# Attention's sixteen units set among the last pieces of the second block's input projection

## What is computed

```
h = rms_norm(x, g_mix_norm) * (1 + sc_m) + sh_m
proj = h @ w_in                       # 1024 -> 5704
q_a, k_a, v_a, q_i, k_i, w_i, q_b, k_b, v_b, gate_a, gate_b = split(proj)
q_a, k_a, q_b, k_b = rope(rms_norm(per head));  q_i, k_i = rope(...)
# DSA, 4 heads of 128: an indexer (8 heads of 64) scores each pair of tokens,
score = sum_h w_i[h] * relu(q_i[h] . k_i), causal;  keep the 64 best keys of each query
o_a = softmax(q_a k_a^T / sqrt(128) over the kept keys) v_a
# MoBA, 4 heads of 128: with 256 tokens there is one block, so it is plain causal attention
o_b = softmax(q_b k_b^T / sqrt(128), causal) v_b
merged = sigmoid(gate_a) * (o_a @ w_br_dsa) + sigmoid(gate_b) * (o_b @ w_br_moba)
x = x + gt_m * (merged @ w_out)
```

## Time and profile before

| | us |
|---|---|
| median of 3 runs | 1394.65 |
| the runs | 1391.75, 1394.65, 1402.45 |
| profiled execution, span from the first to the last instruction | 1392.0 |

### The profile page before, as it was taken

The page is one execution under the profiler, slowest core; times in us unless marked ns, Lnnn a source line. Parts: engine busy times, 40 slices in busy tenths (PEclk is TensorE's granted clock), DMA queues, the critical chain, the costliest instruction groups (busy, mean ns, idle before and its releaser), DMA issues. The chain is left out here.

```text
span 1392.0 us, 19967 instructions
## 1 busy us (share of the span) xinstructions
PE 1208.7 (87%) x7750; PEld 830.8 (60%) x7750; DVE 960.6 (69%) x2109; ACT 413.6 (30%) x879; POOL 276.3 (20%) x264
## 2 busy tenths in 40 slices
PE   4898998888888888888887777779999979999998
PEld 1887866654332423333242222338889869999998
DVE  0595336699787868878786875677776979566552
ACT  2661225321110111111001010136354464544431
POOL 0000000045344444434434343410000000000000
PEclk9899999989999999999999999999999989999999
DMA  9366069699999999999999999974656704566553
GB/s 394 154 235 192 8 243 429 276 410 419 421 421 421 422 421 421 422 420 414 421 411 415 421 402 423 420 323 194 242 189 235 285 18 152 212 235 244 188 201 132
DMA packets 50764, 428.29 MB, mean 308 GB/s; under 512 B 5744, under 2 KB 7920, under 8 KB 8304
## 3 DMA queue, kind: packets, MB, share of 16 engines
q0 software_dynamic: 36864, 268.45, 46.6%
q1 hardware_dynamic: 13808, 158.59, 29.3%
HBM read 423.64 MB, written 1.05 MB: 305 GB/s over the span
## 5 line engine op out<-in xcount | busy, mean ns | idle before, releaser
L1475 PE MATMUL bank<-arena 128*128 128x512 f32 x1024 | 497.7, 615 | 112.2 <-DVE arena L1646 111.8
L1475 PEld LDWEIGHTS bank<-arena 128*128 128x128 f32 x1024 | 177.4, 190 | 417.1 <-DVE arena L1646 274.5
L1710 DVE CUSTOM_DVE_ANT_0 arena<-arena 128x1024 f32<-128x1024 f32 x256 | 313.3, 1224 | 133.6 <-DMA arena<-experts_in,arena 132.5
L1380 POOL DMA_INDIRECT arena<-experts_in,arena x256 | 275.8, 1077 | 605.8 <-PE bank L1475 350.8
L562 PE MATMUL bank<-rounded,rounded 128*128 128x256 f32 x1264 | 372.5, 295 | 26.5 <-DVE rounded L519 13.5
L563 PE MATMUL bank<-rounded,rounded 128*128 128x256 f32 x1264 | 361.6, 286 | 0.0
L564 PE MATMUL bank<-rounded,ring_r 128*128 128x256 f32 x1264 | 361.2, 286 | 0.0
L537 DVE TENSOR_TENSOR ring_r<-ring,rounded 128x1024 fp32r<-128x1024 f32 (+2 forms) x155 | 194.6, 1263 | 113.1 <-ACT rounded L532 112.2
L562 PEld LDWEIGHTS bank<-rounded,rounded 128*128 128x128 f32 x1264 | 246.3, 195 | 34.9 <-issue 25.9
L563 PEld LDWEIGHTS bank<-rounded,rounded 128*128 128x128 f32 x1264 | 246.1, 195 | 3.8 <-issue 3.3
L564 PEld LDWEIGHTS bank<-rounded,ring_r 128*128 128x128 f32 x1264 | 246.0, 195 | 0.0
(11 more groups left out here) (282 smaller groups left out, 994.4 us busy)
## 6 DMA issues: line engine op xcount, KB each, us to landing
ring<-slots_in SPq DMA_DIRECT2D x68, 2048.0 KB, 8.5
arena<-slots_in SPq DMA_DIRECT2D x4, 2048.0 KB, 23.8
arena<-experts_in,arena POOLq DMA_INDIRECT x256, 13.6
xT<-xT_in SPq DMA_DIRECT2D x1, 1024.0 KB, 10.9
...
```

The lines of the kernel that those rows point to most:

```text
L1380: pool.indirect_dma_start(rows[:, r % GRING, :], None, experts_in, bass.IndirectOffsetOnAxis(ap=expert[:, tt, at:at + 1], axis=0)).then_in ...
L1475: ins = pe.matmul(psum[2 * tt + half][:, :], diag[:, r % DIAGS, :], rows[:, r % GRING, D + 512 * half:D + 512 * half + 512], start=(h == 0 ...
L1710: dve.tensor_tensor_reduce(rows[:, r % GRING, 0:D], rows[:, r % GRING, 0:D], utok[:, tt, :], 1.0, 0.0, ALU.mult, ALU.add, hdot[:, r:r + 1] ...
```

## The change

- The items are in another order: the indexer's q, k and weights first, then DSA's values, DSA's q, MoBA's values, DSA's k, MoBA's q and k; the gates stay last (27 to 42). Which columns of the weights lie in which slot is changed to match.
- The loop over items becomes a loop over 44 slices (45 on ACT). Index scores run in slices 9 to 16, the rounds of top-8 in slices 18 to 25, and the mask is made at the end of slice 25.
- Attention's block is gone. Unit u (DSA's are first now) has its logits in PE's slice 25+u, largest on DVE and exponents on ACT in slice 26+u, scaling and transpose in slice 27+u, copy and values in slice 28+u, and the last copy in slice 29+u.
- Items rotate through three banks (before four), all other products through five (before four).
- The gates are evicted with a plain copy. Behind the last item, Sigmoid is applied in place in two instructions of 128x2048. The branch block's DVE waits for them.
- The attention's result goes to `uT`, so that two copies of 128x1024 between `mixT` and `uT` (L1978, L2197) are gone. The first three pieces of the branch weights are prepared in slices 40 to 42.

```diff
-        items = [item("feat", 0, i * P, qk[:, i, :]) for i in range(4)]
-        items += [item("feat", 1, i * P, qk[:, 4 + i, :]) for i in range(4)]
+        items = [item("feat", 0, i * P, qki[:, i, :]) for i in range(4)]
+        items += [item("feat", 1, 0, qki[:, 4, :])]
+        items += [item("weight", 1, tt, wi[:, tt, :], scale=IDX_SCALE) for tt in range(TT)]
         items += [item("token", 2, tt, vtok[:, 0, tt, :]) for tt in range(TT)]
-        items += [item("feat", 3, i * P, qki[:, i, :]) for i in range(4)]
-        items += [item("feat", 4, 0, qki[:, 4, :])]
-        items += [item("weight", 4, tt, wi[:, tt, :], scale=IDX_SCALE) for tt in range(TT)]
-        items += [item("feat", 5, i * P, qk[:, 8 + i, :]) for i in range(4)]
-        items += [item("feat", 6, i * P, qk[:, 12 + i, :]) for i in range(4)]
-        items += [item("token", 7, tt, vtok[:, 1, tt, :]) for tt in range(TT)]
-        items += [item("feat", 8 + i // 4, (i % 4) * P, sgate[:, i, :], ACT.Sigmoid) for i in range(16)]
+        items += [item("feat", 3, i * P, qk[:, i, :]) for i in range(4)]
+        items += [item("token", 4, tt, vtok[:, 1, tt, :]) for tt in range(TT)]
+        items += [item("feat", 5, i * P, qk[:, 4 + i, :]) for i in range(4)]
+        items += [item("feat", 6, i * P, qk[:, 8 + i, :]) for i in range(4)]
+        items += [item("feat", 7, i * P, qk[:, 12 + i, :]) for i in range(4)]
+        items += [item("feat", 8 + i // 4, (i % 4) * P, sgate[:, i, :]) for i in range(16)]
...
+        score, left, relu = uT[:, 0:2, :], uT[:, 2:4, :], uT[:, 4:8, :]
+        maskd, max8 = area(27692, TT, T), area(28204, TT, 8)
+        NI = 16
+        nmax, psm, rsm = area(28220, NI), area(28236, NI), area(28252, NI)
+        sm, pT = area(21792, 4, T), area(4096, 2, T)
...
+        LAST_OF = [10, 12, 16, 18, 20, 22, 24, 26]
+        SUM_AFTER = {LAST_OF[p] + 1: p for p in range(NPAIR)}
+        ROOT_AFTER = {LAST_OF[p] + 2: p for p in range(NPAIR)}
+        NORM_AT = {LAST_OF[p] + 3: p for p in range(NPAIR)}
+        FLIP_AFTER = {2: 8, 4: 9, 6: 10, 14: 0, 16: 1, 20: 2, 22: 3, 24: 4, 26: 5, 28: 6, 30: 7}
+        TURN_AT = {4: 8, 6: 9, 8: 10, 16: 0, 18: 1, 22: 2, 24: 3, 26: 4, 28: 5, 30: 6, 32: 7}
         TURNS = [TURN_AT[t] for t in sorted(TURN_AT)]
-        DOTS = {5: (0, 1), 6: (1, 2), 8: (2, 4), 12: (4, 6), 13: (6, 8), 22: (8, 10), 25: (10, 12), 29: (12, 13),
-                30: (13, 14), 31: (14, 15), 32: (15, 16), 33: (16, 17), 34: (17, 18), 35: (18, 19), 36: (19, 20)}
-        FIRST_SCORE = 29
-        AUX = {}
-        for n in range(NITEM):
+        QI_EVICTED = {8: 2, 9: 4, 10: 5}
+        DOTS = {5: (0, 1), 6: (1, 2), 7: (2, 3), 9: (3, 4), 10: (4, 6), 11: (6, 8)}
+        DOTS.update({26 + j: (8 + j, 9 + j) for j in range(12)})
+        FIRST_SCORE, FIRST_ROUND, FIRST_UNIT = 9, 18, 25
+        AUX_BANK, NAUX = 3, 5
...
+        def what(u):
+            b, h, tt = u // 8, u // 2 % 4, u % 2
+            return b, h, tt, width[tt]
+        wbr = Split([(SLOTS["w_br"][0] + n // 8, D, (n % 8) * P, n) for n in range(16)], 4, uT, 22816, sem("br_mm"),
+                    x_at=17696)
+        br_mm = wbr.mm
...
+                def logits(u):
+                    b, h, tt, w = what(u)
+                    bank = aux_bank("logit", u)
+                    pe.wait_ge(hr["fin"], TURNS.index(4 * b + 2 + h // 2) + 1)
+                    pe.matmul(bank[:, 0:w], qk[:, 8 * b + h, tt * P:(tt + 1) * P], qk[:, 8 * b + 4 + h, 0:w],
+                              start=True, stop=True).then_inc(at["s"], 1)
+
+                def shares_turned(u):
+                    b, h, tt, w = what(u)
+                    bank = aux_bank("turn", u)
+                    pe.wait_ge(at["p"], u + 1)
+                    for st_ in range(tt + 1):
+                        ins = pe.transpose(bank[:, st_ * P:(st_ + 1) * P], sm[:, u % 4, st_ * P:(st_ + 1) * P], ident)
+                    ins.then_inc(at["t"], 1)
+
+                def values(u):
+                    b, h, tt, w = what(u)
+                    bank = aux_bank("value", u)
+                    pe.wait_ge(at["pT"], u + 1)
+                    for st_ in range(tt + 1):
+                        ins = pe.matmul(bank[:, 0:P], vtok[:, b, st_, h * HD:(h + 1) * HD],
+                                        pT[:, u % 2, st_ * P:(st_ + 1) * P], start=(st_ == 0), stop=(st_ == tt))
+                    ins.then_inc(at["o"], 1)
...
+                for n in range(PLAIN, NSLICE):
+                    if n < NITEM:
+                        kind, s, col, *_ = items[n]
+                        if items[n - 1][1] != s:
+                            wait_slot(pe, W2[s])
+                        if n >= 3:
+                            pe.wait_ge(i2_ev, n - 2)
+                        bank, w = psum[n % 3], slot(W2[s])
...
+                    u = n - FIRST_UNIT
+                    if 0 <= u < NI:
+                        logits(u)
+                    if 0 <= u - 2 < NI:
+                        shares_turned(u - 2)
+                    if 0 <= u - 3 < NI:
+                        values(u - 3)
...
+                def exponents(u):
+                    w = what(u)[3]
+                    act.wait_ge(at["max"], u + 1)
+                    act.activation(sm[:, u % 4, 0:w], sm[:, u % 4, 0:w], ACT.Exp, bias=nmax[:, u:u + 1],
+                                   accum_out=psm[:, u:u + 1]).then_inc(at["exp"], 1)
+
+                def shares_out(u):
+                    w = what(u)[3]
+                    act.wait_ge(at["t"], u + 1)
+                    if u >= 2:
+                        act.wait_ge(at["o"], u - 1)
+                    act.copy(pT[:, u % 2, 0:w], aux("turn", u)[:, 0:w]).then_inc(at["pT"], 1)
+
+                def values_out(u):
+                    b, h, tt, w = what(u)
+                    act.wait_ge(at["o"], u + 1)
+                    act.copy(uT[:, 4 * b + h, tt * P:(tt + 1) * P], aux("value", u)[:, 0:P]).then_inc(at["oT"], 1)
 
                 mix2_norm.act(act, wi2, rooted=True, late=True)
-                for n, (kind, s, col, dst, func, scale) in enumerate(items):
-                    if n >= PLAIN and n + LEAD in i2_feat:
+                for n in range(NSLICE + 1):
+                    if PLAIN <= n and n + LEAD in i2_feat:
                         wi2.act_hi(act, i2_feat.index(n + LEAD) - PLAIN)
-                    act.wait_ge(i2_mm, n + 1)
-                    if n == NITEM - 1 or items[n + 1][1] != s:
-                        act.sem_inc(slot_used[W2[s] % RING], 1)
-                    of = {"feat": T, "token": CH, "weight": HEADS}[kind]
-                    act.activation(dst, psum[n % 4][:, 0:of], func, scale=scale).then_inc(i2_ev, 1)
+                    u = n - FIRST_UNIT
+                    if 0 <= u - 1 < NI:
+                        exponents(u - 1)
+                    if 0 <= u - 3 < NI:
+                        shares_out(u - 3)
+                    if 0 <= u - 4 < NI:
+                        values_out(u - 4)
+                    if n < NITEM:
+                        kind, s, col, dst, func, scale = items[n]
+                        act.wait_ge(i2_mm, n + 1)
+                        if n == NITEM - 1 or items[n + 1][1] != s:
+                            act.sem_inc(slot_used[W2[s] % RING], 1)
+                        of = {"feat": T, "token": CH, "weight": HEADS}[kind]
+                        act.activation(dst, psum[n % 3][:, 0:of], func, scale=scale).then_inc(i2_ev, 1)
                     if n in LAST_OF:
                         squares(LAST_OF.index(n))
                     if n in ROOT_AFTER:
                         roots_of(ROOT_AFTER[n])
-                    if n in (1, 3):
-                        act_token(act, 2, n // 2)
+                    if n in (1, 2):
+                        act_token(act, 2, n - 1)
                     if n in (2, 3):
                         act.wait_ge(wide_mm, n - 1)
                         act.copy(wide[:, 512 * (n - 2):512 * (n - 1)], psum[7][:, :]).then_inc(wide_out, 1)
-                    if n == 18:
-                        act.copy(uT[:, 0:4, :], mixT[:, 4:8, :])
-                    if n in (19, 20):
-                        act_token(act, 7, n - 19)
+                    if n in (9, 10):
+                        act_token(act, 4, n - 9)
                     if FIRST_SCORE < n <= FIRST_SCORE + HEADS:
                         positive(2 * (n - FIRST_SCORE) - 2)
                         positive(2 * (n - FIRST_SCORE) - 1)
+                    if 40 <= n < 43:
+                        wbr.act_prime(act, n - 40, n - 39)
+                    if n == NITEM:
+                        act.wait_ge(i2_ev, NITEM)
+                        act.activation(sgate[:, 0:8, :], sgate[:, 0:8, :], ACT.Sigmoid).then_inc(gate_ready, 1)
+                act.activation(sgate[:, 8:16, :], sgate[:, 8:16, :], ACT.Sigmoid).then_inc(gate_ready, 1)
...
+                def selection():
+                    dve.wait_ge(ix_top, 4 * (DSA_TOPK // 8))
```

(66 more changed lines are left out.)

204 lines of the change are left out of this document (54 added, 150 removed).

## The result

The kernel after takes 1416.45 us (median of 4 runs, 1412.95 to 1419.01), the kernel before 1397.61 us (4 runs, 1391.75 to 1402.45). The ratio is 1.0134, with a 95% interval of 1.0107 to 1.0161: slower by some 15 to 22.5 us. Forecast were 1401.6 us and a range up to 1412; the measured time lies outside it. The profiled run took 1414.19 us, 2.59 above its span of 1411.6.

A forecast was written before the change was run, and what follows sets the result against it. From slice 26 a loop through ACT and DVE was to bound the kernel. With 5.3 us of ring stalls the branch starts at 1145.7 instead of 1138.74 (+7.0): span 1399.0, plus 2.65 gives 1401.6 us, range 1385 to 1412.

The forecast's parts named there:

- Up to slice 25: Stretch before attention's units: a small shift, PE's slice 25 beginning at about 1048.2 instead of 1055.55 less 5.72 and 1.34.
- the step I trusted least: The sum up to slice 25, where twenty steps were moved; named, with the landing times, as the likeliest error.
- From slice 26 a loop through ACT and DVE sets the pace.: Slices 26 to 38: each costs ACT's and DVE's lists summed, 4.55 us, whatever PE does; 62.8 us in all.
- Slices with a turn are bound by DVE's own list: Slices 26, 28, 30 and 32 take 5.4 us each; with last roots on ACT, 3.6 us more in all.
- The ring: ACT's waits for DMA at items 35 and 39: stalls of 2.7 and 2.6 us, costing 5.3; bounds 0 and 8.
- The tail: Behind the last product: eviction, piece, copies, table load 1.28 and two Sigmoids of 1.9 us; sum 6.6 us.
- The table loads: Rival: Exp and Ln mixed in slices 26 to 28 take up to four loads of 1.28 us; 1406, chance 0.08.
- The clock: Second rival: PE's granted clock falls behind the loop's and ring's waits, 1.6 us per fall; +17, 1411; chance 0.16.
- The first rival: PE stays the bound and attention hides as meant: -13.3 us, 1381.4; chance 0.12 fully, 0.06 in part (about 1392).

The follow-up runs named there:

- c_units_first: The kernel after, with DVE doing the units' scaling and largest ahead of the low part in each slice; 1408.07 us, ratio to before 1.0079.
- a_flip_bank: The kernel after, with flips from flip 6 on kept in flip 5's bank and other products rotating through four; 1405.17 us, ratio to before 1.0049.
- b_turn_next: The kernel after, with the turns of pairs 5, 6 and 7 one slice behind their flips instead of two; 1405.41 us, ratio to before 1.0071.
- k_order_alone: c_units_first plus R, with banks, turns, dots and Sigmoids as in the kernel after; 1402.32 us, ratio to before 1.0026.
- g_four: The kernel after with the edits of a_flip_bank, b_turn_next, c_units_first and f_sigmoid_late together; 1393.04 us, ratio to before 0.9969.
- R: An edit: from slice 26 ACT rounds the coming part behind its eviction, DVE makes the low part a slice later; in k_order_alone 1402.32 us.
- m_best: l_no_dots with the first Sigmoid in slice 41 and the second behind the branch block's fifth piece; 1387.18 us, ratio to before 0.9927.
- f_sigmoid_late: The kernel after, with both Sigmoids moved into the branch block behind ACT's rounding of pieces 5 and 8; 1415.62 us, ratio to before 1.0123.
- l_no_dots: g_four plus R, with the dots left as in the kernel after; 1385.73 us, ratio to before 0.9903.

## Why the prediction was wrong

**Up to slice 25.** Right within 2 us. DVE enters slice 26 at 1053.26 - 948.79 = 104.5 us into the stage; forecast were 1055.4 - 952.75 = 102.65. The 2.98 us wait went, as forecast, and no other of its kind came; the step I trusted least held.

**"From slice 26 a loop through ACT and DVE sets the pace."** This is the step that failed, in its slices with turns. Forecast for slices 26 to 38, with both ring stalls, 62.8 + 5.3 = 68.1 us; measured 1133.78 - 1053.26 = 80.5: **12.4 of the 14.8 us** by which the branch's start was missed (the rest: 1.8 up to slice 26, 0.6 in the tail). In parts:
- Slices 33 to 38: 29.3 us with one ring stall, forecast 6 x 4.55 + 2.6 = 29.9. The exponents at 1106.90, 1111.43 and 1115.93 are 4.53 and 4.50 us apart, forecast 4.55. Here the loop is what I said, and c_units_first, which opens it, falls to 3.7.
- Slices 26 to 32: 51.2 us, forecast 38.2 with one ring stall. "Slices with a turn are bound by DVE's own list", 5.4 us, holds for 26 and 28 (5.5 and 5.5). It fails for 30 and 32 (11.6 and 10.8), and slice 29 takes 6.5 for 4.55, behind the flip's wait of 1.83 us. That is the rotation of the five banks, shown by a_flip_bank, b_turn_next and k_order_alone. I had written down that the other products rotate through five banks and had priced no wait for one: "so each slice costs the sum of both lists, whatever PE does" left PE out of the loop. With a bank between DVE's turn and PE's transpose, PE's list and ACT's eviction come into the same circle. In a_flip_bank, where the transposes don't wait, the stage takes 196.6 us; the forecast for after was 193.0.

**The ring.** 2.7 and 2.6 us forecast, 2.25 and 2.11 measured. The first reaches PE, as part of its 7.82 us; that both count in full while the loop holds can't be read off one run. They grow as the loop gets faster (4.65 and 3.50 in g_four), and in the kernels with R they are gone or down to 0.19 us (m_best): the rounding then comes later than the load.

**The tail.** Table load 1.28 and Sigmoids of 1.91 us, forecast 1.9. From DVE's slice 39 to the branch's first product 22.8 us, forecast 22.2. The two Sigmoids 2048 wide were well bounded by twice a 1024-wide cast less the fixed part.

**The table loads** of Exp and Ln didn't come. The Trainium skill ("ScalarE: Activation LUTs", "What ACT_TABLE_LOAD costs") gives a switch of tables some 1380 ns of drain besides the load; by that, as an estimate, the tail would have been 1.4 us longer. The trace doesn't have it: the copy ahead of the load ends at 1149.63, the load starts at 1149.65, and the Sigmoid starts at 1150.94. So the measurement decides against it here.

**The clock,** the second rival (+17, 1411), is near in its number, and right in part. Where PE waits 5.17 and 7.82 us for a bank the granted clock is 0.78; in the window with the second ring stall, where PE waits up to 1.4 us at a time, it is 1.00:

```profile
1068.00:1098.00 30.00, 17.01 (x101) 15.96 (x101) 17.59 (x36) 7.92 (x21) 0.00 (x0) 0.78 0.39 141
...
1110.00:1140.00 30.00, 24.44 (x191) 22.61 (x190) 18.17 (x42) 12.83 (x39) 0.00 (x0) 1.00 0.71 279
```

In the first window PE is idle for 13.0 us of 30. What the clock adds can be read from the stretches in which PE works without a pause behind its four waits of 2.13, 1.83, 5.17 and 7.82 us:

```profile
1060.51:1065.00 4.49, 4.49 (x25) 4.48 (x25) 4.39 (x11) 1.80 (x4) 0.00 (x0) 0.62 0.29 124
1067.03:1072.00 4.97, 4.97 (x23) 4.39 (x24) 4.69 (x9) 2.37 (x6) 0.00 (x0) 0.66 0.00 0
1078.94:1086.00 7.06, 7.06 (x35) 6.93 (x36) 1.23 (x2) 1.40 (x4) 0.00 (x0) 0.61 0.01 3
1097.65:1103.00 5.35, 5.35 (x30) 5.35 (x31) 1.23 (x2) 0.53 (x2) 0.00 (x0) 0.64 0.00 0
```

A part of each stretch runs at the half level (1.2 GHz) and the rest at 2.4 GHz, so the time lost is the length times what the clock lacks to 1: an estimate of 1.7, 1.7, 2.8 and 1.9 us, where the rival had 1.6 for each fall. The last two lie in the turn circles. Of the 6.2 and 5.4 us by which slices 30 and 32 are above their forecast of 5.4, some 2.8 and 1.9 us are thus the clock, and the rest is the circle itself. My sum had the clock at nothing. The rival put the falls down to the loop's own waits and to the ring; what brings the two costly ones on is the rotation of banks, and they go with it in a_flip_bank (1.00 from 1080 to 1110).

The clock also differs between two executions of the same list. Up to the tail f_sigmoid_late has the same instructions as after, and flip 6 waits 1.78 us there and 1.83 in after. From that flip to the end of the next wait, first in after, then in f_sigmoid_late:

```profile
1067.03:1078.94 11.91, 6.74 (x37) 5.97 (x37) 9.53 (x20) 4.18 (x10) 0.00 (x0) 0.80 0.49 176
```

```profile
1069.20:1079.45 10.25, 5.08 (x37) 4.68 (x37) 9.53 (x20) 4.16 (x10) 0.00 (x0) 0.89 0.43 144
```

The same 37 products keep PE busy for 6.74 us in the first and for 5.08 in the second, 1.7 us less. So "about 2 us" of waiting, from which the prediction let this rival count, isn't a limit that these traces bear out: behind nearly the same wait the clock fell in after (0.66 above) and stayed at 1.00 in f_sigmoid_late (1068 to 1076).

**The first rival** (PE bound, -13.3) was rightly given a small chance for this kernel. Its condition, that ACT's rounding doesn't stand ahead of the exponents, isn't enough: k_order_alone meets it and stays slower than before. With the banks mended and the Sigmoids moved as well, l_no_dots has the stage at 177.0 us, 9.0 less than before.
